# Ten tile pairs of the first two feed-forward layers as 2x2 blocks in seven half-size products

## What is computed

```python
def swiglu(x, wi, wo):
    gate, up = jnp.split(x @ wi, 2, axis=-1)
    return (jax.nn.silu(gate) * up) @ wo
...
for li in range(DEPTH):
    h = h + 0.5 * swiglu(rms_norm(h, ffn1_norm[li]), ffn1_wi[li], ffn1_wo[li])
    ...
    h = h + 0.5 * swiglu(rms_norm(h, ffn2_norm[li]), ffn2_wi[li], ffn2_wo[li])
```

## Time and profile before

| what | value |
|---|---|
| median of 3 runs | 2772.65 us |
| the profiled execution's own time | 2773.5 us |
| its span in the profile | 2771.8 us |
| granted TensorE clock, mean of the span | 0.995 |
| TensorE busy | 2718.9 us (98%) |
| VectorE busy | 1577.0 us (57%) |
| ScalarE busy | 1205.8 us (44%) |
| GpSimd busy | 624.0 us (23%) |
| loads from and stores to memory | 255.23 MB, mean 92 GB/s |

### The profile page before, as it was taken

How to read it: one execution, slowest core, us unless ns; L and a number is a source line. 1 busy time by engine, 2 the same in 40 slices (tenths; PEclk the granted TensorE clock), 3 DMA queues, 4 the chain that set the end, 5 groups by cost and what they waited for, 6 DMA issues and landing times.

```text
span 2771.8 us, 39060 instructions
## 1 busy us (share of the span) xinstructions
PE 2718.9 (98%) x14176; PEld 2210.0 (80%) x14176; DVE 1577.0 (57%) x2453; ACT 1205.8 (44%) x1814; POOL 624.0 (23%) x607
## 2 busy tenths in 40 slices
PE   8999999999999999999899999999999999899998
PEld 6888888788888888887778888877888888777777
DVE  5444336544443575435865764338777777676664
ACT  4333232443322333223553333236655555457775
POOL 3000013100001451003733530014322222123232
PEclk9999999999999999999999999999999999999999
DMA  5333332233333564333203653322222222122222
...
DMA packets 484826, 255.23 MB, mean 92 GB/s; under 512 B 17843, under 2 KB 478422, under 8 KB 484710
## 3 DMA queue, kind: packets, MB, share of 16 engines
...
q10 hardware_dynamic: 176, 0.27, 0.0%
...
## 4 chain that ended last, share of the span: by engine, by line
PE 91%; DVE 6%; ACT 1%; POOL 1%; issue 1%; DMA 0%; SPq 0%; DVEq 0%; POOLq 0%; ACTq 0%
PE bank L259 73%; PE bank L1881 2%; PE bank L1912 1%; PE bank L1914 1%; PE bank L1913 1%; DVE dsa_work L1578 1%; DVE w_lo L245 1%; DVE small L1572 1%; PE bank L1988 1%; PE bank L2796 1%; PE bank L2788 1%; PE bank L2025 1%; PE bank L2821 1%; DVE gdn_blocks L2385 1%; PE bank L981 1%
## 5 line engine op out<-in xcount | busy, mean ns | idle before, releaser
L259 PE MATMUL bank<-x_hi,w_hi 128*128 128x512 f32 x2320 | 936.6, 404 | 8.6 <-DVE w_lo L245 4.8
L259 PE MATMUL bank<-x_hi,w_lo 128*128 128x512 f32 x2320 | 907.6, 391 | 0.0
L259 PE MATMUL bank<-x_lo,w_hi 128*128 128x512 f32 x2320 | 906.7, 391 | 0.6 <-DVE x_lo L586 0.6
L245 DVE TENSOR_TENSOR w_lo<-w_raw,w_hi 128x1024 fp32r<-128x1024 f32 x429 | 531.0, 1239 | 556.3 <-ACT w_hi L239 555.7
L239 ACT ACTIVATE w_hi<-w_raw 128x1024 fp32r<-128x1024 f32 x429 | 450.6, 1055 | 621.4 <-PE bank L259 572.1
L259 PEld LDWEIGHTS bank<-x_hi,w_hi 128*128 128x128 f32 x2320 | 437.1, 188 | 106.5 <-issue 16.1
L259 PEld LDWEIGHTS bank<-x_hi,w_lo 128*128 128x128 f32 x2320 | 436.2, 188 | 93.2
L259 PEld LDWEIGHTS bank<-x_lo,w_hi 128*128 128x128 f32 x2320 | 437.5, 189 | 87.5 <-issue 3.6
L435 POOL TENSOR_TENSOR sumsq<-sumsq,sq 128x512 f32<-128x512 f32 x56 | 92.3, 1648 | 1293.0 <-ACT sq L421 1292.4
L259 PE MATMUL bank<-h_hi,w_hi 128*128 128x512 f32 x768 | 298.9, 389 | 1.6 <-DVE h_lo L1612 1.6
L259 PE MATMUL bank<-h_hi,w_lo 128*128 128x512 f32 x768 | 298.8, 389 | 0.0
...
## 6 DMA issues: line engine op xcount, KB each, us to landing
w_raw<-in_ffn_wi_dram SPq DMA_DIRECT2D x176, 512.0 KB, 3.8
w_raw<-in_ffn_wo_dram SPq DMA_DIRECT2D x64, 512.0 KB, 4.1
w_raw<-in_ada_w_dram SPq DMA_DIRECT2D x48, 512.0 KB, 4.9
w_raw<-in_a_w_in_dram SPq DMA_DIRECT2D x48, 512.0 KB, 4.0
w_raw<-in_b_w_in_dram SPq DMA_DIRECT2D x32, 512.0 KB, 4.2
...
w_raw<-in_even_w_in_dram SPq DMA_DIRECT2D x16, 512.0 KB, 4.0
w_raw<-in_a_w_out_dram SPq DMA_DIRECT2D x16, 512.0 KB, 3.4
```

Source lines behind the costliest of these rows:

```text
L245: dve.tensor_tensor(w_lo[s][:], w_raw[raw_of(b) % RAW][:], w_hi[s][:].bitcast(F32), ALU.subtract).then_inc(w_lo_done, 1)
L259: mm = pe.matmul(out, lhs[:, w], rhs(kt), start=first and kk == 0 and m == 0, stop=last and kk == len(kts) - 1 and m == 2)
```

## The change

Pairs 4 to 13 of ffn0 and ffn1 (`SEVEN_AT`, `SEVEN_N`) are no longer two tiles of 24 matmuls with 512 columns. Such a pair is seen as a 2x2 block product. Its weights are W11, W12 (gate, first and last four of the eight slices) and W21, W22 (up); the activations are B11, B12 (first four slices, first and last 256 tokens) and B21, B22. Seven products of half the depth and half the tokens give the four results, each 12 matmuls of 256 columns, so 84 in place of 48.

- Weight sums, on GpSimd, per pair: `w_both` = W11 + W21, then W11 + W21 + W22 and W21 + W22 in place in the weight buffers, and `w_all` = W11 + W21 + W22 + W12; each 128 x 512.
- High parts on ScalarE and rests on VectorE, per pair: W11 alone (`left`), `w_both`, `w_all`, each 128 x 512, and two blocks of 128 x 1024 (`row`, `low`). Each of the five has one place (slots 0, 2, 3 and the two halves of slot 1), which is refilled when the product of the pair before has used it.
- Activation sums, once per layer: ScalarE writes `x_part` from `hres` (8 instructions in the first two pairs), GpSimd makes four differences and sums of 128 x 1024 in it, ScalarE their high parts `t_hi`, VectorE the rests `t_lo`.
- Results: product 1 is copied by ScalarE from bank A to bank B and product 7 to SBUF (`p7_copy`), 128 x 256 each. VectorE joins and scales the quarters in six instructions of 128 x 256 (`last_dve`, `join_dve`, `gate_dve`, `up_dve`).
- Order: TensorE takes for pair n products 6 and 2, then product 3 of pair n - 1, products 1 and 7 of pair n + 1, and products 5 and 4 of pair n. ScalarE and VectorE go by the lists in `seven_act` and `seven_dve`, in which steps of pairs n - 1, n, n + 1 and n + 2 alternate. All of this is written out without a loop.
- SyncE loads the same bytes, but waits for `all_added` and `row_lo` (gate block) and `low_lo` (up block) of two pairs before.

```diff
+SEVEN = (0, 1)
+SEVEN_AT, SEVEN_N = 4, 10
+HT = T // 2
...
+        def seven_group(pe, slot, h, x, out, first=False):
...
+            for k in range(4):
+                w = slice(h * T + k * P, h * T + k * P + P)
+                for m, (lhs, rhs) in enumerate(((hi, x_h), (hi, x_l), (lo, x_h))):
+                    mm = pe.matmul(out, lhs[:, w], rhs[:, k, :], start=first and k == 0 and m == 0, stop=k == 3 and m == 2, skip_group_check=True)
...
+        def seven_pe(pe, f, one):
+            one(7, part=0)
+            first_and_seventh_pe(pe, f, 0, 7)
+            one(7, part=1)
+            for n in range(SEVEN_N):
...
+                pe.wait_ge(row_lo, c + 1)
+                pe.wait_ge(p1_copied, c + 1)
...
+                seven_group(pe, slot_of(f, 0), 0, part_pair(2), B[:, T1])
+                pe.wait_ge(p7_copied, c + 1)
+                seven_group(pe, slot_of(f, 0), 1, own_pair(1, T1), A[:, T1]).then_inc(p2_done, 1)
+                if n:
+                    last_pe(pe, f, n - 1)
+                if n + 1 < SEVEN_N:
+                    first_and_seventh_pe(pe, f, n + 1, 1)
+                    first_and_seventh_pe(pe, f, n + 1, 7)
+                pe.wait_ge(low_lo, c + 1)
+                pe.wait_ge(p7_joined, c + 1)
...
+                seven_group(pe, slot_of(f, 3), 0, part_pair(1), B[:, T1])
+                seven_group(pe, slot_of(f, 3), 1, part_pair(3), B[:, T2]).then_inc(p4_done, 1)
...
+        def seven_act(act, f):
...
+            for n in range(SEVEN_N):
+                if n + 1 < SEVEN_N:
+                    row_act(act, f, n + 1)
...
+                all_act(act, f, n)
+                if n:
+                    seven_silu(act, f, n - 1)
+                if n + 2 < SEVEN_N:
+                    left_act(act, f, n + 2)
+                if n + 1 < SEVEN_N:
+                    copy_act(act, f, n + 1)
+                if n:
+                    seven_h_hi(act, f, n - 1)
+                if n + 1 < SEVEN_N:
+                    low_act(act, f, n + 1)
+                if n + 2 < SEVEN_N:
+                    both_act(act, f, n + 2)
...
+        def last_dve(dve, f, n):
...
+            dve.wait_ge(p4_done, seven(f) + n + 1)
+            dve.tensor_tensor(prod[s][:, T2], B[:, T1], p7_copy[n % 2], ALU.add).then_inc(last_joined, 1)
+            dve.scalar_tensor_tensor(prod[s][:, T1], B[:, T2], -1.0, rstd[:, T1], ALU.mult, ALU.mult).then_inc(tile_free, 1)
...
+        def both_pool(pool, f, n):
...
+            pool.tensor_tensor(w_both[:], w_raw[raw % RAW][:, LEFT_H], w_raw[(raw + 1) % RAW][:, LEFT_H], ALU.add).then_inc(both_added, 1)
+
+        def three_pool(pool, f, n):
+            c, raw = seven(f) + n, raw_of(seven_block(f, n))
+            pool.wait_ge(left_lo, c + 1)
+            pool.wait_ge(both_added, c + 1)
+            pool.tensor_tensor(w_raw[raw % RAW][:, LEFT_H], w_both[:], w_raw[(raw + 1) % RAW][:, RIGHT_H], ALU.add).then_inc(three_added, 1)
+
+        def low_pool(pool, f, n):
...
+            pool.tensor_tensor(w[:, LEFT_H], w[:, LEFT_H], w[:, RIGHT_H], ALU.add).then_inc(low_added, 1)
+
+        def all_pool(pool, f, n):
+            c, raw = seven(f) + n, raw_of(seven_block(f, n))
+            pool.wait_ge(three_added, c + 1)
+            if n:
+                pool.wait_ge(all_lo, c)
+            w = w_raw[raw % RAW]
+            pool.tensor_tensor(w_all[:], w[:, LEFT_H], w[:, RIGHT_H], ALU.add).then_inc(all_added, 1)
```

More of the change, by code:

```diff
@@ L171, in first_and_second_block @@
         stage_rows = [tile(f"stage_rows{k}", 16 + k) for k in range(3)]
+        x_part = tile("x_part", 4, KT)
+        t_hi = [tile(f"t_hi{c}", FT + 14 + 2 * c, 2, F32R) for c in range(4)]
+        t_lo = [tile(f"t_lo{c}", 14 + 2 * c, 2, F32R) for c in range(4)]
+        w_both, w_all = tile("w_both", 13), tile("w_all", FT + 13)
+        p7_copy = [sumsq[:, 0:HT], sumsq[:, HT:T]]
         x_in = tile("x_in", 0, 8)
@@ L198, in first_and_second_block @@
         ada_made, ada_added, ada_summed = sem("ada_made"), sem("ada_added"), sem("ada_summed")
+        part_made, part_added, part_hi, part_lo = sem("part_made"), sem("part_added"), sem("part_hi"), sem("part_lo")
+        left_hi, both_hi, row_hi, low_hi, all_hi = (sem(f"{n}_hi") for n in ("left", "both", "row", "low", "all"))
+        left_lo, both_lo, row_lo, low_lo, all_lo = (sem(f"{n}_lo") for n in ("left", "both", "row", "low", "all"))
+        both_added, three_added, low_added, all_added = (sem(f"{n}_added") for n in ("both", "three", "low", "all"))
+        p1_done, p7_done, p2_done, p3_done, p4_done = (sem(f"p{n}_done") for n in (1, 7, 2, 3, 4))
+        p1_copied, p7_copied, p7_joined, first_taken, last_joined, up_scaled = (
+            sem(n) for n in ("p1_copied", "p7_copied", "p7_joined", "first_taken", "last_joined", "up_scaled"))
         normed = sem("normed")
@@ L627, in ffn_sp @@
             o0 = AHEAD + 4 * turns
+            if f in SEVEN:
+                for o in range(AHEAD, 2 * SEVEN_AT):
+                    own(o)
+                for n in range(SEVEN_N + 2):
+                    at = (SEVEN_AT + n) * P
+                    seven_sp(sp, f, n, lambda m: weight_cols(wi, slice(m * FF + at, m * FF + at + P)))
+                o0 = 2 * (SEVEN_AT + SEVEN_N + 2)
             with sp.Fori(0, (2 * FT - o0) // 4) as i:
@@ L686, in ffn_pe, with one @@
             b0, t0 = BASE[f"ffn{f}"]
-            if not ada_of(f):
+            if f in SEVEN:
+                def one(u, i=0, n=0, part=None):
+                    if not part:
+                        pe.wait_ge(tile_free, t0 + u + 1 + i * n)
+                    products(pe, b0 + u, bank[(t0 + u) % BANKS][:], x_of(x_hi), x_of(x_lo), range(KT), True, True, i, n, part)
+                project_pe(pe, run, b0, t0, 4, r, begun)
+                for u in range(4, 2 * SEVEN_AT - 1):
+                    one(u)
+                first_and_seventh_pe(pe, f, 0, 1)
+                seven_pe(pe, f, one)
+                o = 2 * (SEVEN_AT + SEVEN_N)
+                for u in range(1, 4):
+                    one(o + u)
+                with pe.Fori(1, (2 * FT - o) // 4) as i:
+                    for u in range(4):
+                        one(o + u, i, 4)
+            elif not ada_of(f):
                 project_pe(pe, run, b0, t0, 2 * FT, r, begun)
@@ L719, in ffn_turns, with ffn_act @@
                 body(4 * turns, 4, turns, i, False)
-        def ffn_act(act, f, r, after):
+        def ffn_act(act, f, r, after, gain=None):
             b0, t0 = BASE[f"ffn{f}"]
@@ L732, in turn @@
                     split_hi(act, b0 + o0 + 2 * s + 2 + AHEAD, i, 4, raws)
+                    if f in SEVEN and turn0 == 0:
+                        parts_act(act, f, gain, range(4 * s, 4 * s + 4))
                     act.wait_ge(prod_done, pair + i * 2)
@@ L735, in ffn_act @@
             split_hi(act, b0 + AHEAD)
-            ffn_turns(act, f, turn)
+            if f in SEVEN:
+                for k in range(SEVEN_AT // 2 - 1):
+                    turn(4 * k, 4, k, 0, False)
+                seven_act(act, f)
+                k = (SEVEN_AT + SEVEN_N) // 2
+                with act.Fori(0, FT // 2 - k) as i:
+                    turn(4 * k, 4, k, i, False)
+            else:
+                ffn_turns(act, f, turn)
             down_act(act, b0 + 2 * FT, FT, after, 1)
```

342 lines of the change are left out of this document (339 added, 3 removed).

## The result

| | before | after |
|---|---|---|
| median of 7 runs each on one chip, us | 2772.65 | 2781.35 |
| ratio, 95% interval | | 1.0032 (1.0020 to 1.0044) |
| profiled execution: own time, span, us | 2773.5, 2771.8 | 2781.76, 2779.9 |

The change makes the kernel 8.7 us slower, or 0.32%; the interval leaves out no change. The forecast was 2780 us, +7. The page's first part shows little of it: TensorE has more matmuls and 6 us less busy time, VectorE 131 us more work, GpSimd 164 us more.

What follows compares the result with a forecast made beforehand. The prediction took TensorE's column rate to bound the kernel before, and VectorE's 11.25 us round after. Twice +3.1 us and up to 0.5 per layer for a late `row` gave +7, 2780 us; forecast 2776 to 2785, range 2750 to 2791.

Steps and rivals of the forecast that it cites:

- Now the order: In each pair, GpSimd's additions hold up VectorE's `product`, `left`, `low` and `both`, losing 3.5 us.
- VectorE's own 7.8 us: VectorE's list per pair takes 7.8 us without losses; 3.5 lost makes a round taken as 11.25 (bounds 7.8 to 12.4).
- TensorE's 0.115 us a matmul: In the ten pairs, 256-column matmuls start 0.115 us apart (bounds 0.1135 and 0.120), so 9.66 us per pair.
- before product 7 or 5: In each pair's round TensorE waits some 1.5 us for VectorE, before product 7 (for `both_lo`) or product 5.
- Edges: Start and end of each layer's ten pairs, added to the rounds: stretch of 112.0 us against 108.9, +3.1 per layer.
- are hidden: At each layer's start, GpSimd's some 20 us of long additions lie beside pairs 0 to 3, hidden behind TensorE's 43.5 us.
- up to 0.5 us per layer if the first `row` is late: At the ten pairs of each layer, an extra of up to 0.5 us for a late first `row`.
- TensorE stays the bound: Rival: GpSimd's additions fall beside bank instructions or waits, under 1.9 us lost per pair; 2750 us (2748 to 2757), chance 0.24.
- Half of it: Rival: VectorE loses 2.2 to 3 us per pair, round 10.0 to 10.8; 2757 to 2776 us, chance 0.20.
- More waits: Rival: ScalarE's `copy`, waiting for product 7, closes a ring adding 0.75 us per round; 2791 us, bounds 2800, chance 0.14.
- Nothing but columns counts: Rival: 256-column matmuls take 0.107 us, 8.96 per pair, and VectorE loses nothing; 2736 us, chance 0.04.
- Waits called "issue": Rival: the unrolled program runs short of instructions, eating the gain; no own size, chance counted with "More waits".

Runs made afterwards that it cites:

- Experiment 1: In the changed kernel, GpSimd's four additions per pair became constant fills that read nothing: 2763.95 us, ratio 0.9971.
- experiment 4: In the changed kernel, `join` was put ahead of the subtraction for `both` on VectorE: 2773.59 us, ratio 1.0006.
- experiments 5: In the changed kernel, all four GpSimd additions moved to VectorE from the third pair on, `both`'s behind `left`: 2771.50 us, ratio 0.9995.
- 8: In the changed kernel, later pairs' four additions and the sums of quarters of x moved to VectorE, `join` ahead of `both`: 2765.49 us, ratio 0.9974.
- experiment 12: In the changed kernel, each matmul of 15 ordinary products per layer was split into two of 256 columns: 2791.36 us, ratio 1.0067.

## Why the prediction was right

The mechanism, its place and its size in a round were foreseen. That the total came within 2 us of the forecast is partly luck, as the edges below show.

**The mechanism and the place**: shown. The lengths of `product`, `left`, `low` and `both`, the free ones and the releasers are those of the step "Now the order"; the loss of 0.95 + 1.09 + 0.35 + 1.09 = 3.5 us came as 0.91 + 1.10 + 0.42 + 1.10. Experiment 1 takes the reads away and the loss with them; 4 moves it to where nothing is held.

**VectorE's own 7.8 us**: 7.48. The instructions of 256 columns are spaced 0.33, with a scalar as well, where 0.42 was taken for two of them, and the 0.3 for waits was 0.2 at most. With it the round was 11.00, not 11.25. The bounds of 7.8 to 12.4 held it.

**TensorE's 0.115 us a matmul**: 0.120, the upper bound. The step that failed is the choice of "nearest row": two intervals between isolated short matmuls in the earlier trace rows against the 0.227 of some hundred in a row. The floor was 84 x 0.120 = 10.08, not 9.66, so the wait per round was 0.93 us and not 1.5. It did not move the time, since VectorE set the round, but it cuts what any repair can give against the kernel before by a third: 8.1 us a layer, not 12.3.

**TensorE to wait "before product 7 or 5"**: it waits 0.6 before product 3 (for `last`) and 0.3 before product 7.

**Edges**: errors of size that cancel, by luck. From product 6 of pair 0 to the end of product 4 of pair 9 the forecast had 107.8 us and the profile shows 103.2: 8 x 0.25 = 2.0 less by the rounds, and 2.6 less because VectorE was not as far behind there: two of the first rounds run at 10.08 and 10.64, which is 1.3 us of it, and the other 1.3 is in the first distances and was not followed up. That VectorE had caught up while TensorE waited at the start is argued from this. For "up to 0.5 us per layer if the first `row` is late" the layers' lengths give the rest: 6.4 - 3.1 + 4.6 = 7.9 us in ffn0 and 2.3 - 3.1 + 4.6 = 3.8 in ffn1. The traces show 4.1 us of waiting and 2.8 us lost by the halved clock behind it, and 2.9 us with 0.4 more; 1.0 and 0.5 us are left without a place. The sentence that was wrong is that GpSimd's some 20 us at the start "are hidden": GpSimd's time was hidden, but not what its four long additions do to VectorE, the same hold as in the rounds, at twice the length. 4.6 less and 7.4 and 3.3 more per layer leave the sum near: +8.7 where +7 was forecast.

**The rivals.** *TensorE stays the bound* is what experiments 5 and 8 make of the kernel; the change's order did not. *Half of it* is experiment 4 (this rival's own sum was off: twice -4.5 gives 2764 at the bottom, not 2757). *More waits* did not come: with 0.10 us of idle time in VectorE's round, no ring closed. *Nothing but columns counts* is refuted by experiment 12. Waits called "issue" are 0.4 us, once in a layer.
